# A hybrid decoder layer on one core: in chosen k steps of the plain products, one token half is finished before the other begins

## What is computed

```python
h = x + 0.5 * swiglu(rms_norm(x, g_ffn1), w_ffn1_gu, w_ffn1_down)     # D_FF = 2816
u = rms_norm(h, g_mix)
q, k, v, zg, r, us5 = split(u @ w_in)
mix = concat(GLA(q, k, v, zg) gated by r, S5(us5))                    # gated linear attention; state-space model
h = h + mix @ w_out
h = h + cross_attend(rms_norm(h, g_cross), memory K and V, w_cq, w_co) # 4 heads, 256 memory tokens
h = h + 0.5 * swiglu(rms_norm(h, g_ffn2), w_ffn2_gu, w_ffn2_down)
y = rms_norm(h, g_final)
```

## Time and profile before

| | |
|---|---|
| median of 3 runs | 1280.26 us (1280.12 to 1280.7) |
| the profiled execution | 1278.66 us |
| its span, first to last instruction | 1276.8 us |
| mean granted TensorE clock | 0.996 |
| busy: PE, PEld | 1263.2 us (99%), 1222.8 us (96%) |
| busy: DVE, ACT, POOL | 858.3, 531.3, 354.2 us |
| matmuls, and as many weight loads | 10181 |

### The profile page before, as it was taken

One profiled execution on the slowest core, in us unless ns is written; L12 is line 12 of the kernel. 1 busy time (PEld: TensorE's weight loads), 2 busy tenths in 40 slices (PEclk: granted clock), 3 DMA queues, 4 the chain that ended last, 5 costly groups with the idle time before them and its releaser, 6 DMA issues.

```text
span 1276.8 us, 24146 instructions
## 1 busy us (share of the span) xinstructions
PE 1263.2 (99%) x10181; PEld 1222.8 (96%) x10181; DVE 858.3 (67%) x1062; ACT 531.3 (42%) x803; POOL 354.2 (28%) x411
## 2 busy tenths in 40 slices
PE   8999999999999999999999999999999999999998
PEld 8999999999999999999899997699999999999997
DVE  5986479847985637468565437479995589637953
ACT  7553145421224422574433323246552255314543
POOL 0036633288993211000002100032330133102321
PEclk9999999999999999999999999999999999999998
DMA  6223223263223532125332756322333323322322
GB/s 194 84 83 100 83 86 97 84 137 92 83 62 89 103 82 52 51 83 155 104 100 83 261 195 221 99 83 67 100 100 85 98 83 100 96 82 88 88 63 75
DMA packets 221085, 129.95 MB, mean 102 GB/s; under 512 B 22257, under 2 KB 213281, under 8 KB 220961
## 3 DMA queue, kind: packets, MB, share of 16 engines
q1 hardware_dynamic: 217664, 123.86, 34.1%
q10 hardware_dynamic: 3312, 4.54, 1.1%
HBM read 121.42 MB, written 5.78 MB: 100 GB/s over the span
## 4 chain that ended last, share of the span: by engine, by line
PE 94%; DVE 3%; ACT 1%; issue 1%; DMA 1%; SPq 0%; DVEq 0%; ACTq 0%
PE PS L744 91%; PE PS L1386 1%; DMA raw<-in_w_ffn_gu 1%; ACT gua L1674 0%; PE PS L1472 0%; DVE xl L2159 0%; PE PS L1363 0%; DVE AR L2802 0%; PE PS L976 0%; PE PS L868 0%; ACT Xs L1945 0%; DVE PS L2148 0%; DVE PS L2141 0%; ACT wh L1525 0%; DVE ARr L2154 0%
## 5 line engine op out<-in xcount | busy, mean ns | idle before, releaser
L1525 ACT ACTIVATE wh<-raw 128x1024 fp32r<-128x1024 f32 (+1 forms) x126 | 130.1, 1032 | 375.7 <-PE PS L744 375.0
L744 PE MATMUL PS<-yh,wh 128*128 128x288 f32 x960 | 206.0, 296 | 0.0
L744 PE MATMUL PS<-yh,wl 128*128 128x288 f32 x960 | 205.0, 295 | 0.0
L744 PE MATMUL PS<-yl,wh 128*128 128x288 f32 x960 | 205.0, 295 | 0.0
L2047 DVE TENSOR_TENSOR wl<-raw,wh 128x1024 fp32r<-128x1024 f32 (+1 forms) x126 | 154.9, 1230 | 63.6 <-ACT wh L1525 62.2
L744 PE MATMUL PS<-xh,ARr 128*128 128x288 f32 x792 | 174.2, 297 | 0.4 <-ACT sq L1608 0.2
L744 PE MATMUL PS<-xh,wh 128*128 128x288 f32 x736 | 163.7, 304 | 0.6 <-DVE xl L2359 0.6
L744 PE MATMUL PS<-xh,wl 128*128 128x288 f32 x736 | 157.7, 296 | 0.0
L744 PE MATMUL PS<-xl,wh 128*128 128x288 f32 x736 | 157.3, 295 | 0.0
L744 PEld LDWEIGHTS PS<-yh,wh 128*128 128x128 f32 x960 | 154.1, 188 | 1.5 <-DVE yl L2727 0.8
L744 PEld LDWEIGHTS PS<-yl,wh 128*128 128x128 f32 x960 | 154.4, 188 | 0.0
(11 more groups left out here) (381 smaller groups left out, 2191.5 us busy)
## 6 DMA issues: line engine op xcount, KB each, us to landing
raw<-in_w_ffn_gu SPq DMA_DIRECT2D x88, 512.0 KB, 3.8
raw<-in_w_ffn_down SPq DMA_DIRECT2D x32, 512.0 KB, 4.0
raw<-in_w_in SPq DMA_DIRECT2D x16, 512.0 KB, 4.0
raw<-in_w_ckv SPq DMA_DIRECT2D x16, 512.0 KB, 3.8
raw<-in_w_ffn_down SPq DMA_DIRECT2D x16, 384.0 KB, 3.4
Hs<-in_cache_mem_k SPq DMA_DIRECT2D x6, 1024.0 KB, 6.2
raw<-in_w_out SPq DMA_DIRECT2D x8, 512.0 KB, 4.0
raw<-in_w_cq SPq DMA_DIRECT2D x8, 512.0 KB, 5.2
```

The lines of the kernel that those rows point to most:

```text
L744: return e.matmul(out, lhsT, rhs, start=start, stop=stop, **kw)
L1525: e.activation(wh[:, n % 2, 0:K * P], raw[:, n % 4, 0:K * P], ACT.Copy).then_inc(w_hi, 1)
```

## The change

`dense` gets an argument `by_half`, a tuple of k. In such a k the six matmuls are issued as three for half 0 and then three for half 1. `STEADY` is (0, 1, 6). The tuple is given to the first plain block of a group that has nothing else between its k, and a single k is given in places where other work stands in front. No matmul, wait or hook is added or taken away.

```diff
+        STEADY = (0, 1, 6)
...
-            def dense(n, par, K, xa, xb, width=TH, parts=2, ready=None, inside=None, each=None, ahead=False):
+            def dense(n, par, K, xa, xb, width=TH, parts=2, ready=None, inside=None, each=None, ahead=False, by_half=()):
...
+                def term(i, wi, j):
+                    w, x = ((wh, xa), (wh, xb), (wl, xa))[wi]
+                    return mm(bank(b0 + j, width), w[:, par, i * P:(i + 1) * P], x[:, i, j * width:(j + 1) * width],
+                              start=(i == 0 and wi == 0), stop=(i == K - 1 and wi == 2))
+
                 for i in range(K):
-                    k = i
                     if ready:
                         e.wait_ge(ready[0], ready[1] + i + 1)
-                    for wi, (w, x) in enumerate(((wh, xa), (wh, xb), (wl, xa))):
+                    if i in by_half:
                         for j in range(parts):
-                            last = mm(bank(b0 + j, width), w[:, par, k * P:(k + 1) * P],
-                                      x[:, k, j * width:(j + 1) * width],
-                                      start=(i == 0 and wi == 0), stop=(i == K - 1 and wi == 2))
+                            for wi in range(3):
+                                last = term(i, wi, j)
+                    else:
+                        for wi in range(3):
+                            for j in range(parts):
+                                last = term(i, wi, j)
...
-            def dense_group(gi, xa, xb, ready=None, in_first=None, **kw):
+            def dense_group(gi, xa, xb, ready=None, in_first=None, steady=False, **kw):
...
-                    dense(g["n0"], 0, g["K"], xa, xb, ready=ready, inside=in_first and (in_first, KD - 3), **kw)
+                    dense(g["n0"], 0, g["K"], xa, xb, ready=ready, inside=in_first and (in_first, KD - 3),
+                          by_half=STEADY if steady else (), **kw)
...
-                    dense(g["n0"] + i, i % 2, g["K"], xa, xb, **kw)
+                    dense(g["n0"] + i, i % 2, g["K"], xa, xb, by_half=STEADY if steady and i == 0 else (), **kw)
...
                     dense(groups[gi]["n0"] + b, b % 2, groups[gi]["K"], yh, yl, ready=(hid_lo, groups[gi - 1]["f0"]) if b == 0 else None,
-                          each=each if b == KD - 1 else None)
+                          each=each if b == KD - 1 else None,
+                          by_half=(STEADY[:2] if b == 0 else STEADY[:1] if b == 1 else ()) if groups[gi]["K"] < KD else STEADY if b == 0 else ())
...
-            dense(2, 0, KD, xh, xl, inside=(spread_roots, 0), ahead=True)
+            dense(2, 0, KD, xh, xl, inside=(spread_roots, 0), ahead=True, by_half=(3,))
...
-                dense(n, n % 2, KD, xh, xl)
+                dense(n, n % 2, KD, xh, xl, by_half=STEADY if n == 4 else ())
...
-            dense_group(4, xh, xl)
+            dense_group(4, xh, xl, steady=True)
...
                       inside=(lambda: rms(1), KD - 3) if b == 0 else None, each=lambda i: beside(b, i),
+                      by_half=(0,) if b == 1 else (1,) if b == 9 else ())
...
-                dense(n0 + i, i % 2, KD, yh, yl)
+                dense(n0 + i, i % 2, KD, yh, yl, by_half=(0,) if i == 2 else ())
...
-            dense(n0 + 1, 1, KD, xh, xl)
+            dense(n0 + 1, 1, KD, xh, xl, by_half=(0,))
...
-                dense(n0 + i, i % 2, KD, xh, xl, each=turn_kv if i == 2 else None)
+                dense(n0 + i, i % 2, KD, xh, xl, each=turn_kv if i == 2 else None, by_half=STEADY if i == 3 else ())
...
-            dense_group(W_O, yh, yl, ready=(S("pv_lo"), 0))
+            dense_group(W_O, yh, yl, ready=(S("pv_lo"), 0), steady=True)
...
-            dense(n0 + 1, 1, KD, xh, xl)
+            dense(n0 + 1, 1, KD, xh, xl, by_half=(0,))
```

More of the change, by code:

```diff
@@ L1115, in _ @@
                 dense(n0 + b, b % 2, KD, xh, xl, ready=(x_lo, 8) if b == 0 else None,
-                      inside=(lambda: rms(1), KD - 3) if b == 0 else None, each=lambda i: beside(b, i))
+                      inside=(lambda: rms(1), KD - 3) if b == 0 else None, each=lambda i: beside(b, i),
+                      by_half=(0,) if b == 1 else (1,) if b == 9 else ())
             TURN_K = (6, 7, 1, 3, 6)
```

## The result

The changed kernel took **1271.86 us** (median of 5 runs, 1271.34 to 1272.91) against 1280.26 before (1279.48 to 1280.7): ratio 0.9939 with an interval of 0.9925 to 0.9952, 8.4 us less. The forecast was 1269.0. The profiled execution took 1272.91 us, its span is 1271.1. That is 5.8 us less than the profiled one before, not 8.4. By the start times of the matmuls it was already 0.9 us behind at 46 us, made up 7.4 from there to the last matmul, and lost 0.7 again behind it: in the trace of before the last output transfer is issued 3.0 us ahead of the end of the span, in this one 3.7.

What follows compares the result with a forecast made beforehand. TensorE's matmul pace was taken as the bound: 3474 matmuls × 3.33 ns = 11.6 us, taken as −11.3, from the 1280.26 median to 1269.0. Likeliest case 1267.5 to 1271; the range also holds 1279 to 1281 and leaves out rival 3.

Steps and rivals of the forecast that it cites:

- The windows that were to show it: First down group, group 4 and the group at 1105 us should hold 369 matmuls in 48 us, not 360.
- only k 6 does it: Alternative in groups with k 0, 1 and 6: first block still at 133.3; seven groups lose 36 matmuls each, 0.8 us.
- rival 1: Plain blocks: nothing locks, the stream settles at 133.3 again and the time stays, 1280.3; chance 0.29.
- rival 3: Plain blocks behind a by-half k settle above 133.3; +11.6 us over all 3474 matmuls, 1291.9; chance 0.07.
- The waits, which were to stay: PE's waits should stay as they are, while its busy time falls with the span.
- What comes after it: Plain matmuls behind each kick: by-half k bring the product's pace, then 130.0 until the next disturbance; 3474 matmuls, 11.6 us.
- rival 2: Only some kicks work: single-k places stay at 133.3, those with k 0, 1 and 6 lock; −7.8, 1272.4; chance 0.17.
- single k: Places with one by-half k (6 matmuls): the matmuls behind each were counted as going at 130.0.
- group 5: Has no kick, follows group 4 without a break, so its 288 matmuls were counted at 130.0.
- last down group: From its second block to its seventh, 210 matmuls were counted at 130.0.
- the group at 966 us: Already at 130.0, so counted as gaining nothing; rival 1 said it may lose its 1.3 us.
- Cost 0; if the cover were gone at 44 us, at most that stretch's 0.6 us.: Suppliers at 130.0, tightest at 44 to 68 us: DVE still fits; otherwise the price is at most 0.6 us.

Runs made afterwards that it cites:

- k01_alone: The changed kernel with STEADY = (0, 1), so k 6 is in plain order again; 1276.41 us (one run).
- by_phase: The changed kernel with, instead of its bursts, at most one by-half k per stream, placed behind the long step in the earlier trace; 1273.16 us, ratio 0.9952.
- k6_alone: The changed kernel with STEADY = (6,), so k 0 and 1 are in plain order again; 1273.92 us (one run).
- changed_again: The changed kernel unaltered, measured and profiled a second time; 1270.47 us, ratio 0.9935.
- HALF_1_FIRST: Down group at 1105 us, every k halves alternating, half 1 first, in a run giving the changed kernel's whole groups other orders; 1274.09 us (one run).
- changed_third: The changed kernel unaltered, measured once more beside the last two kernels; 1270.81 us, ratio 0.9935.
- resync: The changed kernel with bursts reset in block 2, behind s5_turn, in group 5 and the last down group, and none in group 4; 1270.94 us, ratio 0.9939.
- X_TURNS: Group at 961 us, every k halves alternating, products reordered, in a run giving the changed kernel's whole groups other orders; 1274.09 us (one run).
- LAST_KIND: Down group at 1105 us, k 6 by half with products reordered, in a run giving the changed kernel's k 6 other orders; 1275.11 us (one run).

## Why the prediction came out as it did

**Right.** Two steady paces of the same stream, 3.33 ns apart, kept until the next disturbance, are what bounds the plain blocks, and the order of a few matmuls moves a stream from one to the other. The windows that were to show it do, with the same clock, and the first block runs at 133.3 up to k 6, the sign that the forecast gave for "only k 6 does it". Nothing locks (rival 1) and slower (rival 3) are refuted by them. The waits, which were to stay, did not quite (below). A rule by columns alone, as the Trainium skill has it (TensorE: Matmul & The Clock Gate, Back-to-back issue gap), can't tell 302 from 309 matmuls in the same 40 us of the same group (k01_alone, by_phase).

**Wrong: the step "What comes after it"**, by which k 0 and 1 set the product's rhythm and so leave the stream at 130.0. They leave it slow (k01_alone: all their groups at 133.3, and the fast one at 966 us lost). What makes it fast is the third k, if it begins behind the long step; k 0 and 1 only see to it that it does. The change had that k; the prediction gave no reason for it, kept it as a way out at a price of 0.8 us, and in rival 1 even as a danger. So the number came near partly by luck, and rival 2's 1272.4, nearer still, is luck too: its single k were to fail, and in the result's profile none of W_IN's, W_OUT's, W_Q's, FFN2's and block 2's did. (W_Q's second block failed in k6_alone and by_phase, block 2 in three profiles, FFN2's in changed_again.)

The premise of that step holds. By the start times of all profiles, plain order with half 0 first that came out of products at 3.19 us for 24 was fast from the entry, 3 of 3: before, the first down group of k6_alone, and the group at 962 us of by_phase, which had no burst. Out of products at 3.16 us it was slow, 15 of 15.

```profile
110.15 0.43 PE L745 MATMUL PS<-ARr,xh 128*128 128x288 f32 x2
...
113.34 0.43 PE L745 MATMUL PS<-yh,wh 128*128 128x288 f32 x2
```

These are k6_alone's, 3.19 us. What fails is the transfer: behind k 0 and 1 by half plain order is slow in all 57 pairs, also where the products ahead went at 3.19 us (six of them, after's at 114 and 961 us among them). And HALF_1_FIRST was fast out of products at 3.16 us, where half 0 first was slow each time.

**The terms of the sum**, in matmuls at 130.0 ns that were at 133.3, by the start times in the trace:

| place | forecast | measured |
|---|---|---|
| seven stretches behind (0, 1, 6): blocks 4 to 7, three down groups, group 4, W_Q, W_O | 180 + 372 + 180 + 564 + 228 + 408 + 372 | 30 less in each: 2094 |
| single k: blocks 2 and 3, W_IN, W_OUT, W_Q, FFN2 | 672 | 672 |
| group 5 | 288 | 0 |
| last down group | 210 | 0 |
| the group at 966 us | 0 | −42 |
| sum | 3474 | 2724 |

2724 × 3.33 ns is 9.1 us, 2.5 less than the 11.6 that the forecast added up (of which it took 11.3):
- *30 in each of seven*: it is k 6, not k 1, that starts it. The forecast had this as its alternative (36 in each, 0.8 us) and took a part of it.
- *Group 5*: it was to go on at the pace of group 4. It does, until a chunk of the activations comes late. The wait that broke it is new:

```profile
383.69 0.42 PE L745 MATMUL PS<-yh,wl 128*128 128x288 f32 x2
384.51 0.53 PE L745 MATMUL PS<-yh,wh 128*128 128x288 f32 x2 [0.41 <-DVE yl L2265]
```

  These pairs start 0.82 us apart instead of 0.26, and behind the wait the stream is slow: 218 in 29 us. In changed_again and changed_third the pairs at this place come only 0.1 us late, no wait is listed, and the stream is slow behind it all the same.
- *Last down group*: its (0, 1) and (0) are in two blocks with a wait between, behind which the rhythm wasn't settled: the second block's first matmul starts at 1221.25 us, 0.32 behind the one before it instead of 0.13. resync, with both moved one block later, has it fast.
- *The group at 966 us* loses 42 while k 0 and 1 throw it out and k 6 brings it back. The forecast counted it at nothing, though rival 1 named it.

**"Cost 0; if the cover were gone at 44 us, at most that stretch's 0.6 us."** The cover was gone, and the whole price was paid: blocks 4 to 7 save 150 × 3.33 = 0.5 us, and by the start times the changed kernel gives back 0.6 between 66 and 87 us. Half of it stands ahead of the second unit's fifth product, where PE waits for ACT's copy out of the banks. PE was late there already before, too little for the list of waits: it stood idle for 0.07 us (85.25 and 0.95, then 86.27), now for 0.38. The other half stands ahead of the first unit's fourth product, at 74 us, and no wait is listed for it: 13 matmuls took 1.88 us before, and 15 now take 2.42, 0.27 more than the two added matmuls account for. In each place the lines of before stand first:

```profile
85.25 0.95 PE L744 MATMUL PS<-ARr 128*128 128x288 f32 x6
86.27 0.40 PE L744 MATMUL PS<-xh,ARr 128*128 128x288 f32 x1
...
85.29 1.61 PE L745 MATMUL PS<-ARr 128*128 128x288 f32 x11
87.28 0.40 PE L745 MATMUL PS<-xh,ARr 128*128 128x288 f32 x1 [0.38 <-ACT sq L1620]
...
72.80 1.88 PE L744 MATMUL PS<-ARr 128*128 128x288 f32 x13
...
72.42 2.42 PE L745 MATMUL PS<-ARr 128*128 128x288 f32 x15
```

The wait for ACT is 0.4 us also in k6_alone, changed_again and changed_third, whose blocks 4 to 7 were fast too; in k01_alone, with only blocks 2 and 3 fast ahead of it, it is 0.2, and in before and by_phase it is too short to be listed. So what these blocks save, the first two units give back: PE had no cover left there, and the supplier that showed in the list is ACT, not DVE as the forecast had it. With group 5's delay, 0.1 to 0.6, it is 0.7 to 1.2 us that the forecast had at nothing. The sum is then 9.1 less that, **7.9 to 8.4 us**; 8.4 is measured in the medians (6.1 to 9.6 by the interval), and from 46 us to the last matmul 7.4 in the profiled pair, 7.9 in changed_again and 8.5 in changed_third.

## What to carry to other kernels

A dense stream of matmuls can have more than one steady pace with the same code, shapes and clock: count matmuls in windows of two equal groups, and if they differ, look at the distances of their starts before looking for a stall. Which pace it keeps can be set by the order of six matmuls, if that order comes in the right phase; ahead of it goes something that fixes the phase, for a place read off one trace isn't the same in the next execution. And a quicker stretch pays only as far as its suppliers follow: here 0.7 to 1.2 us of 9.1 came back as waits a few microseconds later.

## What the runs showed of the hardware

- The stream of 288-column products, each matmul with its own weight load, went at 129.9 to 130.0, 131.1 to 131.7, 132.5, 133.3 and 134.2 ns with the clock at 1.00, by the order in which the two token halves and the products follow each other, by which half is read, and by how the stream was entered.
- At 133.3 the starts are 131, 131, 132, 140 ns apart; at 130.0 they are 128, 132. The extra time of the slow pace is one step of 140 in four.
- Twelve matmuls by half put the 140 in a fixed place (57 of 57); six by half, half 0 first, behind a 140 remove it (82 of 82), six elsewhere do not (24 of 24).
- Plain order out of products at 3.19 us for 24 is fast from the entry (3 of 3), out of products at 3.16 slow (15 of 15).
- Whether the halves go to one PSUM bank or to two makes no difference (300 in 40 us with either), and in the two cases tried another order of the products didn't either (X_TURNS, LAST_KIND). Reading one half of the activations twice does (131.6 ns).
- **Open**: why the order of the halves matters, and why half 0 must come first in a burst. What is read of the activations is left as a candidate; no run separated their addresses from the rhythm of the reads. That half 1 first in every k is fast from the entry was seen once, and wasn't tried again. Why the products of a unit come to its end at 3.19 or at 3.16 us for 24 wasn't looked into. Nor is it settled why resync's median isn't below changed_again's: 0.9 us of span separate their profiles, and the phases of the single bursts, the wait at the start (1.2 to 1.9 us in the profiles of the changed kernel), the clock in the first and last matmuls and the time behind the last one (4.3 to 5.4 us) differ from execution to execution by as much.
